# Stationary blocks of the expert stage stored column by column in interleaved rows

## The chip, the cores and the metric

The kernel runs on one core of one Trainium2 chip. The metric is the device time of one execution in microseconds, median of several runs; lower is better. One core has five engines with queues of their own: TensorE (PE, its weight loads listed apart as PEld), VectorE (DVE), ScalarE (ACT), GpSimd (POOL) and SyncE (SP), which here issues the large DMAs.

## What is computed

Two layers of a streaming encoder on 320 tokens (256 of a prompt, 64 of running streams), model width 1024. Each layer is a mixer (gated linear attention, a short convolution and differential attention, all fed by one projection) followed by a feed-forward part; the first layer's is dense, the second's is a mixture of eight experts, two for each token:

```python
D_MODEL, D_FF, N_EXPERTS, TOP_K, D_FF_E = 1024, 2816, 8, 2, 3584

def hybrid_layer(x, ...):
    xn = rmsnorm(x, g_mix)
    qa, ka, va, ga, ra, bb, cb, hb, qc, kc, vc = split_cols(xn @ w_in)
    ...
    x = x + jnp.concatenate([y_a, y_b, y_c], axis=-1) @ w_out
    x = x + ffn(rmsnorm(x, g_ffn))

def moe_ffn(x, w_r, wg, wu, wd):
    ...
    for e in range(N_EXPERTS):
        h = jax.nn.silu(xt @ wg[e]) * (xt @ wu[e])
        y = y + gates[:, e:e + 1] * jnp.dot(h, wd[e], preferred_element_type=F32)
```

All inputs and weights are float32.

## The kernel before, in words

**Precision.** A float32 product is made from three fast products (type `fp32r`, called FR in the code): each operand is split into a high part, which is the value rounded to that type, and a low part, which is the rest, and high x high, low x high and high x low are added in PSUM.

**The two halves of the program.** The first 570 us are the two mixers and the dense feed-forward part. There the weights are the stationary operand (128x128 blocks of `cut_hi` and `cut_lo`) and the 320 tokens stream past them. From about 577 us on, the experts run: there up to 128 tokens of one expert are stationary and the weights stream past them, 512 columns in one matmul.

**The expert stage.** One expert's weights come in 42 pieces (`NP`) of 128 x 2048 words: 28 of gate and up, then 14 of down. The program goes through experts in pairs, eight experts in all, 336 pieces. The SP queue fetches a piece (1 MB) into one of seven slots of `raw`; ACT writes the high part of it to one of three slots of `split_hi`; DVE writes the low part to `split_lo` and so frees the slot of `raw`; TensorE does 12 matmuls of 512 columns with it and then frees the slot of `split_hi` and `split_lo` for the piece three further on. Each of the 12 matmuls is preceded by the load of its 128x128 stationary block.

**The stationary blocks.** These are four tiles:

- `xgT_hi`, `xgT_lo`: the expert's tokens, transposed, in 8 blocks (`KB`) of 128 features. TensorE transposes the gathered rows `xg`, ACT writes each block of the high part with the gain (L1255), DVE the low part (L1823), 128 columns an instruction.
- `hmT_hi`, `hmT_lo`: the expert's activations, transposed, in 28 blocks (`FEB`). TensorE transposes four blocks at a time out of `hm` (L2528), ACT copies the 512 columns (L1303), DVE writes the low part (L1952).

```python
        hmT_hi = sb("hmT_hi", [P, FEB, P], FR)
        xgT_hi = sb("xgT_hi", [P, KB, P], FR)
        TE.matmul(o, xgT_hi[:, kk, :], hi[:, ...], start=kk == 0, stop=False)                          # L2475
        last = TE.transpose(tb[n % 2][:, 128 * k:128 * k + 128], hm[:, m % 2, k:512:4], ident)         # L2528
```

So the 128 columns of one stationary block stand side by side, 128 words in a row, in all four tiles. The transposes of `hm` are different: each takes every fourth column of `hm` as its stationary operand, while the transposes of `xg` (L1984) take 128 columns side by side.

**Lines.** Gate and up: L2475 is high block x high weights, L2479 low block x high weights, L2484 high block x low weights (and L2489 in the first piece). Down: L2510, L2513 and L2519 in the same sense, and L2495, L2496 and L2502 for an expert's last piece. Four instructions of the first part of the program are named further down: `warm`, 20 bfloat16 matmuls of 512 columns at the start; `xR,wr`, the router's product, whose stationary block has 8 columns; `Gown,x`, the first gather, float32 with 128 columns; and L1981, the weights of the first half.

**Order.** Each engine's order is written out by hand; a piece's steps wait on counters (`hi_ready`, `lo_ready`, `piece_used`, `t_full`, `th_ready`, `t_free`). TensorE is asked for a block of `hmT` four pieces before it needs it.

Of the kernel before, what the change touches and what calls it, by code (L numbers as in the profile page):

```python
# [25 lines left out]
P = 128  # L26
# [222 lines left out]
def build(nc, A, O):  # L249
# [5 lines left out]
    with ExitStack() as ctx:  # L255
# [162 lines left out]
        token_rows.close()  # L418
        hmT_hi = sb("hmT_hi", [P, FEB, P], FR)
        ye = sb("ye", [P, D])  # L420
# [36 lines left out]
        xg = sb("xg", [P, D])  # L457
        xgT_hi = sb("xgT_hi", [P, KB, P], FR)
        xgT_lo = sb("xgT_lo", [P, KB, P], FR)
        hs = sb("hs", [P, 2, 512])  # L460
# [3 lines left out]
        last_hot = sb("last_hot", [P, NT * P], FR)  # L464
        sb("below_hmT_lo", [P, 384])
        loop_only = ExitStack()
        hmT_lo = sb("hmT_lo", [P, FEB, P], FR, loop_only)
        loop_only.close()
# [96 lines left out]
        HALVES = [slice(0, 512), slice(512, 1024)]  # L565
        last_y_hi = xgT_hi[:].rearrange("p k n -> p (k n)")
        last_y_lo = xgT_lo[:].rearrange("p k n -> p (k n)")

# [315 lines left out]
        def _(act):  # L884
# [364 lines left out]
            def xg_hi(base, first, ks=range(KB)):  # L1249

                for k in ks:
                    if k % 4 == 0:
                        act.wait_ge(t_full, base + k // 4 + 1)
                    b = tb[(first + k // 4) % 2]
                    last = nc.scalar.activation(xgT_hi[:, k, :], b[:, 128 * (k % 4):128 * (k % 4) + 128], ACT.Copy, scale=gcol(3)[:, k:k + 1])  # L1255
                    if k % 4 == 3:
                        last.then_inc(th_ready, 1)
# [16 lines left out]
            def experts(count, ip, done):  # L1274

                for i in range(done, count * NP):
# [51 lines left out]
        def _(dve):  # L1328
# [488 lines left out]
            def xg_lo(first, base, ks=range(KB)):  # L1817

                for k in ks:
                    if k % 4 == 0:  # L1820
                        dve.wait_ge(th_ready, base + (first + k // 4 + 1))
                    b = tb[(first + k // 4) % 2]
                    last = V.scalar_tensor_tensor(out=xgT_lo[:, k, :], in0=b[:, 128 * (k % 4):128 * (k % 4) + 128], scalar=gcol(3)[:, k:k + 1],  # L1823
                                                  in1=xgT_hi[:, k, :].bitcast(F32), op0=ALU.mult, op1=ALU.subtract)
                    if k % 4 == 3:
                        last.then_inc(t_free, 1)
# [101 lines left out]
            def experts(count, ip, done):  # L1928

                for i in range(done, count * NP):  # L1930
# [45 lines left out]
        def _(pe):  # L1976
# [462 lines left out]
            def experts(count, ip, first=False):  # L2439

                for i in range(count * NP):
# [27 lines left out]
                    if j < 2 * FC:  # L2469
                        n, w = 4 // len(ms), 512 * len(ms)  # L2470
                        outs = [banks[2 * up + (FC * h + m) % 2][:] for m in ms]
                        for k in range(n):
                            kk = n * s + k
                            for c, o in enumerate(outs):
                                TE.matmul(o, xgT_hi[:, kk, :], hi[:, w * k + 512 * c:w * k + 512 * c + 512], start=kk == 0, stop=False)  # L2475
                            if first and i == 0:
                                continue
                            for c, o in enumerate(outs):
                                TE.matmul(o, xgT_lo[:, kk, :], hi[:, w * k + 512 * c:w * k + 512 * c + 512], start=False, stop=False)  # L2479
                        pe.wait_ge(lo_ready, ip * (2 * NP) + (i + 1 + PR))  # L2480
                        for k in range(n):
                            kk = n * s + k
                            for c, o in enumerate(outs):
                                last = TE.matmul(o, xgT_hi[:, kk, :], lo[:, w * k + 512 * c:w * k + 512 * c + 512], start=False, stop=kk == KB - 1)  # L2484
                        if first and i == 0:
                            pe.wait_ge(t_free, 1)
                            for k in range(n):
                                for c, o in enumerate(outs):
                                    last = TE.matmul(o, xgT_lo[:, k, :], hi[:, w * k + 512 * c:w * k + 512 * c + 512], start=False, stop=False)  # L2489
                    elif q == NP - 1:  # L2490
                        for n in range(2):
                            for k in range(2):
                                b = FEB - 2 + k
                                c = slice(1024 * k + 512 * n, 1024 * k + 512 * n + 512)
                                TE.matmul(banks[6 + n][:], hmT_hi[:, b, :], hi[:, c], start=False, stop=False)  # L2495
                                TE.matmul(banks[6 + n][:], hmT_lo[:, b, :], hi[:, c], start=False, stop=False)  # L2496
                            if n == 0:
                                pe.wait_ge(lo_ready, ip * (2 * NP) + (i + 1 + PR))
                            for k in range(2):
                                b = FEB - 2 + k  # L2500
                                c = slice(1024 * k + 512 * n, 1024 * k + 512 * n + 512)
                                last = TE.matmul(banks[6 + n][:], hmT_hi[:, b, :], lo[:, c], start=False, stop=k == 1)  # L2502
                            if n == 0:
                                last.then_inc(left_done, 1)
                    else:
                        for k in range(2):
                            b = 4 * (j - 2 * FC) + 2 * half + k
                            for n in range(2):
                                c = slice(1024 * k + 512 * n, 1024 * k + 512 * n + 512)
                                TE.matmul(banks[6 + n][:], hmT_hi[:, b, :], hi[:, c], start=b == 0, stop=False)  # L2510
                            for n in range(2):
                                c = slice(1024 * k + 512 * n, 1024 * k + 512 * n + 512)
                                TE.matmul(banks[6 + n][:], hmT_lo[:, b, :], hi[:, c], start=False, stop=False)  # L2513
# [93 lines left out]
```

## Time and profile before

| | |
|---|---|
| median of 3 runs | 1537.97 us (1537.42 to 1539.92) |
| the profiled execution, first to last instruction | 1535.8 us |
| PE busy | 1527.8 us, 99% of the span |
| DVE busy | 1234.4 us, 80% |
| ACT busy | 998.9 us, 65% |
| granted TensorE clock, mean | 0.997 |
| pieces of expert weights | 336 |
| matmuls recorded | 8428 |

The profile is of one execution. Its span runs from the first to the last instruction; it is 2.2 us shorter than the median of the runs, which also hold the start and the end of the program. PE's busy time counts overlapping matmuls once. The start of one matmul and the start of the next are what tells the pace; a single matmul is listed with about 390 ns because it is pipelined.

### The profile page before, as it was taken

To read this page: it belongs to the slowest core of one execution; us is meant where nothing else is said; L and a number is where in the kernel's file an instruction comes from. 1 tells how busy PE (TensorE), PEld (TensorE's weight loads), DVE (VectorE), ACT (ScalarE), POOL (GpSimd) and SP (SyncE) were. 2 spreads that over 40 slices of the span, in tenths; PEclk is the share of its full clock that TensorE was granted. 3 is DMA by queue.
4 is the path that set the end of the run, shared out by engine and by line. 5 is a ranking of instruction groups with operands and counts; after the bars stand their busy time and mean duration, and the time that the engine had idled before them with its cause. 6 is when DMAs were issued, how large, how long until landed. Compare 5 with 4: busy or idle time off the path is not lost.

```text
span 1535.8 us, 21611 instructions
## 1 busy us (share of the span) xinstructions
PE 1527.8 (99%) x8428; PEld 1333.0 (87%) x8428; DVE 1234.4 (80%) x1253; ACT 998.9 (65%) x1079; POOL 217.5 (14%) x249
## 2 busy tenths in 40 slices
PE   9999999999999999999999999999999999999998
PEld 7989999999998988888888888888888888888887
DVE  5877666654477758988988888998998988898897
ACT  5655433333466547777777778777777777777775
POOL 5514400001150403101001001002002002002000
PEclk9999999999999999999999999999999999999999
DMA  8333455444443459999999999999999999999994
GB/s 226 96 110 116 149 164 164 133 157 151 125 122 110 141 209 367 383 366 388 372 381 376 374 374 376 391 359 386 384 363 382 381 362 379 400 361 363 394 373 183
DMA packets 159701, 437.43 MB, mean 285 GB/s; under 512 B 12068, under 2 KB 66176, under 8 KB 145264
## 3 DMA queue, kind: packets, MB, share of 16 engines
q1 hardware_dynamic: 151796, 423.02, 75.0%
q0 software_dynamic: 5552, 9.62, 2.3%
q10 hardware_dynamic: 2252, 3.41, 0.7%
q8 instruction: 68, 1.11, 0.3%
q14 instruction: 33, 0.27, 0.1%
HBM read 429.40 MB, written 13.60 MB: 288 GB/s over the span
## 4 chain that ended last, share of the span: by engine, by line
PE 98%; DMA 0%; ACT 0%; DVE 0%; issue 0%; SPq 0%; DVEq 0%; ACTq 0%
PE bank L1981 34%; PE bank L2475 13%; PE bank L2484 13%; PE bank L2479 13%; PE bank L2510 6%; PE bank L2513 6%; PE bank L2519 6%; PE bank L1984 3%; PE bank L2528 2%; PE bank L2496 0%; PE bank L2502 0%; PE bank L2495 0%; DMA gla<-b_g 0%; DVE x L1972 0%; ACT L1076 0%
## 5 line engine op out<-in xcount | busy, mean ns | idle before, releaser
L1808 DVE TENSOR_TENSOR split_lo<-raw,split_hi 128x2048 fp32r<-128x2048 f32 x336 | 763.1, 2289 | 101.8 <-ACT split_hi L1207 100.8
L1207 ACT CAST split_hi<-raw 128x2048 fp32r<-128x2048 f32 x336 | 640.5, 1911 | 224.5 <-PE bank L2484 145.7
L2475 PE MATMUL bank<-split_hi,xgT_hi 128*128 128x512 f32 x896 | 291.7, 395 | 0.0
L2479 PE MATMUL bank<-split_hi,xgT_lo 128*128 128x512 f32 x892 | 285.8, 390 | 0.0
L2484 PE MATMUL bank<-split_lo,xgT_hi 128*128 128x512 f32 x896 | 239.9, 390 | 0.0
L913 ACT CAST cut_hi<-ring 128x1024 fp32r<-128x1024 f32 x124 | 129.9, 1048 | 166.6 <-PE bank L1981 166.6
L1981 PE MATMUL bank<-xT_hi,cut_hi 128*128 128x320 f32 x752 | 236.7, 315 | 0.0
L1981 PE MATMUL bank<-xT_hi,cut_lo 128*128 128x320 f32 x752 | 233.5, 310 | 0.0
L1981 PE MATMUL bank<-xT_lo,cut_hi 128*128 128x320 f32 x752 | 231.9, 308 | 0.0
L1346 DVE TENSOR_TENSOR cut_lo<-ring,cut_hi 128x1024 fp32r<-128x1024 f32 x124 | 153.0, 1235 | 80.7 <-ACT cut_hi L913 79.9
L2484 PEld LDWEIGHTS bank<-split_lo,xgT_hi 128*128 128x128 f32 x896 | 168.3, 188 | 34.9
L2479 PEld LDWEIGHTS bank<-split_hi,xgT_lo 128*128 128x128 f32 x892 | 167.7, 188 | 34.7
L2475 PEld LDWEIGHTS bank<-split_hi,xgT_hi 128*128 128x128 f32 x896 | 166.2, 189 | 32.3
L1981 PEld LDWEIGHTS bank<-xT_hi,cut_hi 128*128 128x128 f32 x752 | 142.1, 189 | 1.6
L1981 PEld LDWEIGHTS bank<-xT_lo,cut_hi 128*128 128x128 f32 x752 | 142.2, 189 | 0.0
L1981 PEld LDWEIGHTS bank<-xT_hi,cut_lo 128*128 128x128 f32 x752 | 142.0, 189 | 0.0
L2510 PE MATMUL bank<-split_hi,hmT_hi 128*128 128x512 f32 x416 | 129.8, 393 | 0.0
L2513 PE MATMUL bank<-split_hi,hmT_lo 128*128 128x512 f32 x416 | 128.3, 390 | 0.0
L2519 PE MATMUL bank<-split_lo,hmT_hi 128*128 128x512 f32 x416 | 111.3, 390 | 0.0
L853 POOL COPY idc<-idx 128x1 uint32 (+1 forms) x8 | 5.7, 707 | 635.9 <-PE bank L1984 616.0
L2513 PEld LDWEIGHTS bank<-split_hi,hmT_lo 128*128 128x128 f32 x416 | 78.2, 188 | 16.3
L2519 PEld LDWEIGHTS bank<-split_lo,hmT_hi 128*128 128x128 f32 x416 | 78.1, 188 | 16.2
(316 smaller groups left out, 1723.2 us busy)
## 6 DMA issues: line engine op xcount, KB each, us to landing
raw<-moe_w_gate SPq DMA_DIRECT2D x112, 1024.0 KB, 7.8
raw<-moe_w_up SPq DMA_DIRECT2D x112, 1024.0 KB, 7.6
raw<-moe_w_down SPq DMA_DIRECT2D x112, 1024.0 KB, 7.3
ring<-w_in SPq DMA_DIRECT2D x15, 1024.0 KB, 5.5
ring<-ffn_w_gate SPq DMA_DIRECT2D x11, 1024.0 KB, 5.5
ring<-ffn_w_up SPq DMA_DIRECT2D x11, 1024.0 KB, 5.4
ring<-ffn_w_down SPq DMA_DIRECT2D x10, 1024.0 KB, 5.1
ring<-w_out SPq DMA_DIRECT2D x8, 1024.0 KB, 5.0
```

The source lines that it names most:

```text
L913: nc.scalar.copy(split_cut(cut_hi, q), raw_cut(q)).then_inc(cut_hi_ready, 1)
L1207: return nc.scalar.copy(split_hi[:, i % SR, :], raw_piece(i)).then_inc(hi_ready, 1)
L1346: V.tensor_tensor(split_cut(cut_lo, q), raw_cut(q), split_cut(cut_hi, q).bitcast(F32), ALU.subtract).then_inc(cut_lo_ready, 1)
L1808: V.tensor_tensor(split_lo[:, i % SR, :], raw_piece(i), split_hi[:, i % SR, :].bitcast(F32), ALU.subtract).then_inc(lo_ready, 1)
L1981: return TE.matmul(out, lhsT, rhs, start=start, stop=stop)
L1984: return TE.transpose(out, in_, ident[0:rows, 0:rows])
L2475: TE.matmul(o, xgT_hi[:, kk, :], hi[:, w * k + 512 * c:w * k + 512 * c + 512], start=kk == 0, stop=False)
L2479: TE.matmul(o, xgT_lo[:, kk, :], hi[:, w * k + 512 * c:w * k + 512 * c + 512], start=False, stop=False)
L2484: last = TE.matmul(o, xgT_hi[:, kk, :], lo[:, w * k + 512 * c:w * k + 512 * c + 512], start=False, stop=kk == KB - 1)
L2510: TE.matmul(banks[6 + n][:], hmT_hi[:, b, :], hi[:, c], start=b == 0, stop=False)
L2513: TE.matmul(banks[6 + n][:], hmT_lo[:, b, :], hi[:, c], start=False, stop=False)
L2519: last = TE.matmul(banks[6 + n][:], hmT_hi[:, b, :], lo[:, c], start=False, stop=b == FEB - 1)
```

## The change

The four tiles of stationary blocks become two, and the two axes of each are exchanged: the index of the block is now the inner one. `spread` has 128 rows of 62 words; words 0 to 7 of a row are column n of the eight blocks of `xgT_hi`, words 8 to 15 those of `xgT_lo`, words 16 to 43 those of the 28 blocks of `hmT_lo`, and 18 words of each row are not used. `spread_hi` has 128 rows of 30 words, 28 of which are column n of the blocks of `hmT_hi`. A load of a stationary block so takes 128 words that stand 62 or 30 words (248 or 120 bytes) apart. ACT and DVE write the blocks, and DVE reads the high ones back, with the same distances. The numbers of instructions, their order on every engine, their semaphores and the operands' sizes stay the same; only names and addresses differ. `last_y`, which lay over `xgT_hi` and `xgT_lo`, gets a tile of its own.

```diff
-        hmT_hi = sb("hmT_hi", [P, FEB, P], FR)
+        spread_hi = sb("spread_hi", [P, P, 30], FR)
...
-        xgT_hi = sb("xgT_hi", [P, KB, P], FR)
-        xgT_lo = sb("xgT_lo", [P, KB, P], FR)
+        last_y = sb("last_y", [P, 2, D], FR)
...
-        hmT_lo = sb("hmT_lo", [P, FEB, P], FR, loop_only)
+        spread = sb("spread", [P, P, 62], FR, loop_only)
...
+        def xgT_hi(k):
+            return spread[:, :, 0 + k]
+
+        def xgT_lo(k):
+            return spread[:, :, 8 + k]
+
+        def hmT_hi(b):
+            return spread_hi[:, :, 0 + b]
+
+        def hmT_lo(b):
+            return spread[:, :, 16 + b]
+
+        HMT_HI, HMT_LO = (spread_hi, 0), (spread, 16)
+
+        def four(part, j):
+            tile, first = part
+            return tile[:, :, first + 4 * j:first + 4 * j + 4].rearrange("p n s -> p s n")
+
+        def four_in(bank):
+            return bank[:].rearrange("p (s n) -> p s n", s=4)
...
-                    last = nc.scalar.activation(xgT_hi[:, k, :], b[:, 128 * (k % 4):128 * (k % 4) + 128], ACT.Copy, scale=gcol(3)[:, k:k + 1])
+                    last = nc.scalar.activation(xgT_hi(k), b[:, 128 * (k % 4):128 * (k % 4) + 128], ACT.Copy, scale=gcol(3)[:, k:k + 1])
...
-                        nc.scalar.copy(hmT_hi[:, 4 * j:4 * j + 4, :].rearrange("p b n -> p (b n)"), tb[n % 2][:]).then_inc(th_ready, 1)
+                        nc.scalar.copy(four(HMT_HI, j), four_in(tb[n % 2])).then_inc(th_ready, 1)
...
-                        V.tensor_tensor(hmT_lo[:, 4 * j:4 * j + 4, :].rearrange("p b n -> p (b n)"), tb[n % 2][:],
-                                        hmT_hi[:, 4 * j:4 * j + 4, :].rearrange("p b n -> p (b n)").bitcast(F32), ALU.subtract).then_inc(t_free, 1)
+                        V.tensor_tensor(four(HMT_LO, j), four_in(tb[n % 2]), four(HMT_HI, j).bitcast(F32), ALU.subtract).then_inc(t_free, 1)
...
-                                TE.matmul(o, xgT_hi[:, kk, :], hi[:, w * k + 512 * c:w * k + 512 * c + 512], start=kk == 0, stop=False)
+                                TE.matmul(o, xgT_hi(kk), hi[:, w * k + 512 * c:w * k + 512 * c + 512], start=kk == 0, stop=False)
...
-                                last = TE.matmul(banks[6 + n][:], hmT_hi[:, b, :], lo[:, c], start=False, stop=b == FEB - 1)
+                                last = TE.matmul(banks[6 + n][:], hmT_hi(b), lo[:, c], start=False, stop=b == FEB - 1)
```

The other matmuls of the stage change in the same way.

## Rows read from the trace of the kernel before

**Rows 1.** The page: engines' busy us (share of the span) xinstructions
```profile
PE 1527.8 (99%) x8428; PEld 1333.0 (87%) x8428; DVE 1234.4 (80%) x1253; ACT 998.9 (65%) x1079; POOL 217.5 (14%) x249
```

**Rows 2.** The page: chain of work that ended last, shares by line
```profile
PE bank L1981 34%; PE bank L2475 13%; PE bank L2484 13%; PE bank L2479 13%; PE bank L2510 6%; PE bank L2513 6%; PE bank L2519 6%; PE bank L1984 3%; PE bank L2528 2%; PE bank L2496 0%; PE bank L2502 0%; PE bank L2495 0%; DMA gla<-b_g 0%; DVE x L1972 0%; ACT L1076 0%
```

**Rows 3.** The page's groups: operation, count, busy us, mean ns, idle before and releaser
```profile
L1808 DVE TENSOR_TENSOR split_lo<-raw,split_hi 128x2048 fp32r<-128x2048 f32 x336 | 763.1, 2289 | 101.8 <-ACT split_hi L1207 100.8
...
L2475 PE MATMUL bank<-split_hi,xgT_hi 128*128 128x512 f32 x896 | 291.7, 395 | 0.0
...
L2484 PEld LDWEIGHTS bank<-split_lo,xgT_hi 128*128 128x128 f32 x896 | 168.3, 188 | 34.9
```

**Rows 4.** Timeline of PE, 899.9 to 906.2 us: start us, length us, operation
```profile
899.95 0.62 PE L2510 MATMUL bank<-split_hi,hmT_hi 128*128 128x512 f32 x2
...
902.67 0.62 PE L2510 MATMUL bank<-split_hi,hmT_hi 128*128 128x512 f32 x2
```

**Rows 5.** Timeline of PE, 5.95 to 6.0 and 7.60 to 7.62 us
```profile
5.67 0.59 PE L1981 MATMUL bank<-warm 128*128 128x512 bf16 x2
...
7.39 0.38 PE L1981 MATMUL bank<-warm 128*128 128x512 bf16 x1
```

**Rows 6.** Timelines: loads at 561.3 and at 571 us, matmuls at 300 us
```profile
561.32 0.09 PEld L1981 LDWEIGHTS bank<-xR,wr 128*8 128x8 f32 x1 [0.18 <-issue]
...
563.20 0.09 PEld L1981 LDWEIGHTS bank<-xR,wr 128*8 128x8 f32 x1 [0.18 <-issue]
...
570.88 1.20 PEld L1981 LDWEIGHTS bank<-Gown,x 128*128 128x128 f32 x10
...
299.81 0.31 PE L1981 MATMUL bank<-xT_hi,cut_lo 128*128 128x320 f32 x1
...
300.97 0.31 PE L1981 MATMUL bank<-xT_lo,cut_hi 128*128 128x320 f32 x1
```

**Rows 7.** Line L1981: loads by operands, ns min/median/max, first and last start
```profile
L1981 PEld LDWEIGHTS bank<-xT_hi,cut_hi x752: 186/188/331, 14.9 to 527.9; 128*128 128x128 f32 x188
...
L1981 PEld LDWEIGHTS bank<-Gown,x x48: 183/192/193, 570.3 to 576.1; 128*128 128x128 f32 x32, 64*128 64x128 f32 x16
...
L1981 PEld LDWEIGHTS bank<-warm x20: 97/114/152, 1.2 to 7.2; 128*128 128x128 bf16 x20
...
L1981 PEld LDWEIGHTS bank<-xR,wr x18: 85/90/91, 560.8 to 569.6; 128*8 128x8 f32 x18
```

**Rows 8.** Transposes of xg and of hm: timeline around 679 and 905 us
```profile
679.09 1.03 PEld L1984 LDWEIGHTS bank<-const_sb,xg 128*128 128x128 f32 x8
679.32 1.03 PE L1984 MATMUL bank<-const_sb,xg 128*128 128x128 f32 x8
...
905.17 0.67 PEld L2528 LDWEIGHTS bank<-const_sb,hm 128*128 128x128 f32 x4
905.40 0.63 PE L2528 MATMUL bank<-const_sb,hm 128*128 128x128 f32 x4
```

**Rows 9.** Lines L1984 and L2528: those loads and transposes, ns min/median/max
```profile
L1984 PEld LDWEIGHTS bank<-const_sb,xg x64: 138/140/143, 679.1 to 1511.1; 128*128 128x128 f32 x64
L1984 PE MATMUL bank<-const_sb,xg x64: 270/273/273, 679.3 to 1511.2; 128*128 128x128 f32 x64
...
L2528 PEld LDWEIGHTS bank<-const_sb,hm x224: 195/208/220, 604.5 to 1499.3; 128*128 128x128 f32 x112
L2528 PE MATMUL bank<-const_sb,hm x224: 270/283/386, 604.7 to 1499.4; 128*128 128x128 f32 x112
```

**Rows 10.** Groups of 600 to 1500 us: the writers of the blocks
```profile
L1952 DVE TENSOR_TENSOR hmT_lo<-bank,hmT_hi 128x512 fp32r<-128x512 f32 x55 | 37.6, 684 | 0.0
...
L1823 DVE SCALAR_TENSOR_TENSOR xgT_lo<-bank,pcol,xgT_hi 128x128 fp32r<-128x128 f32 x56 | 15.1, 343 | 0.0
```

**Rows 11.** 600 to 1500 us: busy PE, PEld, DVE, ACT, POOL; clock, DMA share, GB/s
```profile
600.00:1500.00 900.00, 899.97 (x4097) 749.72 (x4096) 804.74 (x493) 683.17 (x505) 67.59 (x60) 1.00 1.00 377
```

**Rows 12.** The SP queue's waits, 600 to 1535 us: in total, times, longest us
```profile
SPq L648 <- DVE split_lo L1808: 785.1, 320, 3.9
```

More of the change, by code:

```diff
@@ L464, in build @@
         last_hot = sb("last_hot", [P, NT * P], FR)
-        sb("below_hmT_lo", [P, 384])
+        sb("below_spread", [P, 320])
         loop_only = ExitStack()
-        hmT_lo = sb("hmT_lo", [P, FEB, P], FR, loop_only)
+        spread = sb("spread", [P, P, 62], FR, loop_only)
         loop_only.close()
@@ L565, in build @@
         HALVES = [slice(0, 512), slice(512, 1024)]
-        last_y_hi = xgT_hi[:].rearrange("p k n -> p (k n)")
-        last_y_lo = xgT_lo[:].rearrange("p k n -> p (k n)")
+        last_y_hi, last_y_lo = last_y[:, 0], last_y[:, 1]
+        def xgT_hi(k):
[12 more added lines that the diff above has]
+            return bank[:].rearrange("p (s n) -> p s n", s=4)
         def y_rows_of(t, c):
@@ L1822, in xg_lo @@
                     b = tb[(first + k // 4) % 2]
-                    last = V.scalar_tensor_tensor(out=xgT_lo[:, k, :], in0=b[:, 128 * (k % 4):128 * (k % 4) + 128], scalar=gcol(3)[:, k:k + 1],
-                                                  in1=xgT_hi[:, k, :].bitcast(F32), op0=ALU.mult, op1=ALU.subtract)
+                    last = V.scalar_tensor_tensor(out=xgT_lo(k), in0=b[:, 128 * (k % 4):128 * (k % 4) + 128], scalar=gcol(3)[:, k:k + 1],
+                                                  in1=xgT_hi(k).bitcast(F32), op0=ALU.mult, op1=ALU.subtract)
                     if k % 4 == 3:
@@ L2478, in experts @@
                             for c, o in enumerate(outs):
-                                TE.matmul(o, xgT_lo[:, kk, :], hi[:, w * k + 512 * c:w * k + 512 * c + 512], start=False, stop=False)
+                                TE.matmul(o, xgT_lo(kk), hi[:, w * k + 512 * c:w * k + 512 * c + 512], start=False, stop=False)
                         pe.wait_ge(lo_ready, ip * (2 * NP) + (i + 1 + PR))
@@ L2483, in experts @@
                             for c, o in enumerate(outs):
-                                last = TE.matmul(o, xgT_hi[:, kk, :], lo[:, w * k + 512 * c:w * k + 512 * c + 512], start=False, stop=kk == KB - 1)
+                                last = TE.matmul(o, xgT_hi(kk), lo[:, w * k + 512 * c:w * k + 512 * c + 512], start=False, stop=kk == KB - 1)
                         if first and i == 0:
@@ L2488, in experts @@
                                 for c, o in enumerate(outs):
-                                    last = TE.matmul(o, xgT_lo[:, k, :], hi[:, w * k + 512 * c:w * k + 512 * c + 512], start=False, stop=False)
+                                    last = TE.matmul(o, xgT_lo(k), hi[:, w * k + 512 * c:w * k + 512 * c + 512], start=False, stop=False)
                     elif q == NP - 1:
@@ L2494, in experts @@
                                 c = slice(1024 * k + 512 * n, 1024 * k + 512 * n + 512)
-                                TE.matmul(banks[6 + n][:], hmT_hi[:, b, :], hi[:, c], start=False, stop=False)
-                                TE.matmul(banks[6 + n][:], hmT_lo[:, b, :], hi[:, c], start=False, stop=False)
+                                TE.matmul(banks[6 + n][:], hmT_hi(b), hi[:, c], start=False, stop=False)
+                                TE.matmul(banks[6 + n][:], hmT_lo(b), hi[:, c], start=False, stop=False)
                             if n == 0:
@@ L2501, in experts @@
                                 c = slice(1024 * k + 512 * n, 1024 * k + 512 * n + 512)
-                                last = TE.matmul(banks[6 + n][:], hmT_hi[:, b, :], lo[:, c], start=False, stop=k == 1)
+                                last = TE.matmul(banks[6 + n][:], hmT_hi(b), lo[:, c], start=False, stop=k == 1)
                             if n == 0:
@@ L2509, in experts @@
                                 c = slice(1024 * k + 512 * n, 1024 * k + 512 * n + 512)
-                                TE.matmul(banks[6 + n][:], hmT_hi[:, b, :], hi[:, c], start=b == 0, stop=False)
+                                TE.matmul(banks[6 + n][:], hmT_hi(b), hi[:, c], start=b == 0, stop=False)
                             for n in range(2):
                                 c = slice(1024 * k + 512 * n, 1024 * k + 512 * n + 512)
-                                TE.matmul(banks[6 + n][:], hmT_lo[:, b, :], hi[:, c], start=False, stop=False)
+                                TE.matmul(banks[6 + n][:], hmT_lo(b), hi[:, c], start=False, stop=False)
                         pe.wait_ge(lo_ready, ip * (2 * NP) + (i + 1 + PR))
```

## The prediction

> **What bounds the kernel now.** I read the engines' busy time first [rows 1], then the chain of work that ended last [rows 2], then the groups [rows 3]. PE is busy for 99% of the span, nearly the whole chain is PE's lines, and its expert lines L2475, L2479, L2484, L2510, L2513, L2519 make up 57% of it. No matmul group shows idle time before it. In the expert stage, 600 to 1500 us, PE is busy for 899.97 of 900 us at a granted clock of 1.00, which is 2.4 GHz; DVE is busy for 804.74 us and ACT for 683.17 us [rows 11]. The DMAs wait for DVE to free slots, not the other way round: SP's queue waited 785.1 us for split_lo [rows 12]. So the time of this stage is the number of matmuls times their pace, and only a change of that pace, or something that becomes slower than it, moves the end.
>
> **The pace.** The timeline shows a piece's first matmul at 899.95 us and the next piece's first at 902.67 us, 12 matmuls later [rows 4]: 2.72 / 12 = 226.7 ns each. There are 336 pieces (the count of L1808 [rows 3]), so 336 x 12 = 4032 such matmuls, 914 us of the 1535.8 us of the profiled execution. That execution is 2.2 us under the median of 1537.97 us; I take differences from its rows and put them to the median.
>
> **What the pace consists of.** Streaming 512 columns at one column in a cycle of 2.4 GHz is 213.3 ns, so 13.4 ns of each pitch are something else. Three rows say what kind of thing. (a) The bfloat16 matmuls at the start, 512 columns too, come every (7.39 - 5.67) / 8 = 215 ns [rows 5]; their 128-column loads last 114 ns, where a load of the experts lasts 188 ns [rows 3, 7]. (b) `xR,wr` is a plain float32 matmul of 320 columns with an 8-column load (90 ns [rows 7]) and comes every (563.20 - 561.32) / 7 = 268.6 ns [rows 6], which is two cycles a column, 266.7 ns, plus 2. (c) `Gown,x` is a plain float32 one of 128 columns with a 128-column load of 192 ns [rows 7]: (1.20 - 0.19) / 9 = 112.2 ns [rows 6], two cycles a column, 106.7 ns, plus 5.5. The first half's matmuls, which stream as fast as the experts' and load 128 columns in 188 ns, come every (300.97 - 299.81) / 8 = 145 ns for 320 columns [rows 6, 7]: 133.3 plus 11.7, so the addition does not shrink or grow with the length of the stream. It cannot be a wait for the load, either: at 145 ns the next matmul begins before a load's recorded 188 ns are over, and at 226.7 ns there are 82 ns more. The addition is thus 2 ns with a short or a quick load, 5.5 ns with a full one beside a stream that reads at half pace, and 12 to 13 with a full one beside a stream that reads a word in every cycle. I read this as the load and the stream getting in each other's way in SBUF, some 11 ns for each load; no row shows the collision itself.
>
> **The change, part by part.**
>
> The loads. 4032 loads read 128 words 62 or 30 words apart. What that does to a load that is covered by a stream of 512 columns is the whole question. The address walk is arithmetic. A load of 8 columns lasts 90 ns and one of 128 columns 188 [rows 7], 98 / 120 = 0.82 ns a column, in which time the stream moves by two words. Side by side, the columns move by one word, so the two reads drift against each other and meet again and again. In the first case the distance between the two reads stands still, and at most one collision is left. Neither the banks nor the order of columns is in any row, so I bound the gain: at best the pace becomes that of (a), 215.0 ns, which is 11.7 ns less and 4032 x 11.7 = 47.2 us; at worst it is nothing. I take 217.5 ns, the 215.0 of the quick load plus 2.5 ns, between (a) and (c), since some loads will begin in a bad phase: 9.2 ns x 4032 = 37.1 us.
>
> Against a load being slow in itself: the transposes of `hm` load every fourth column, 4 words apart, those of `xg` side by side, otherwise they are alike. The first last 208 ns at the median and the second 140 [rows 9], and a transpose comes every (630 - 283) / 3 = 116 ns instead of (1030 - 273) / 7 = 108 [rows 8]; the 283 and 273 ns are the lengths of one [rows 9]. So distance makes a load about 68 ns longer. But where such a load lies under a matmul of 512 columns it costs nothing: in both places the last big matmul has the first load beside it, which starts at 905.17 or 679.09, and the first transpose starts 0.23 us later, at 905.40 or 679.32. A load of 188 + 68 = 256 ns whose first 90 ns or so are latency (the 8-column load's 90 [rows 7]) holds its port for about 170 ns, under 217.5. So I cost the length of the loads at nothing; what hides it is the stream, with 48 ns to spare. The Trainium skill, page "SBUF — State Buffer", section "SBUF: two separate sides", holds that lines are 16 bytes and that an access which goes to a new line each time pays a penalty, for float32 from a distance of 4 words on. The longer loads of `hm` agree with it; that the cover takes it up is what those two starts show. Its sections on ports also say that the load and the stream have a read port each and take nothing from each other; by that the 11 ns would not be a collision and the change would give nothing, which is the second rival.
>
> The writers. DVE writes `hmT_lo` 56 times at 684 ns, with its second input spread as well, and `xgT_lo` 64 times at 343 ns [rows 10], where 55 and 56 of them lie in the window. ACT writes the high blocks as often, and has 217 of 900 us free [rows 11]. No row shows DVE or ACT with words so far apart. Bounds: nothing, or each word twice as long, which is 512 x 1.04 = 533 ns more for a `hmT_lo` and 133 for a `xgT_lo` (1.04 ns from L1808: 2289 ns for 2048 words with its fixed part, at most 1.12). That is 56 x 0.53 + 64 x 0.13 = 38 us of DVE in the stage. At today's pace DVE has 900 - 805 = 95 us free there, so it hides; at the new one 58 us are free, and it still does on average. I take nothing. PE asks for a block four pieces (10.9 us) before it uses it, which covers another 0.5 us twice. The added tile `last_y` moves nothing.
>
> What else could be late next. At 217.5 ns a piece takes 2.61 us, and DVE needs 2.29 us of that for the piece alone. The transposes lengthen the round for both. DMA would have to move 377 x 900 / 863 = 393 GB/s instead of 377 [rows 11]. The share of 1.00 there is no limit by itself, since the queue waits for slots; but 4% more is not shown to be free.
>
> Sum: 1537.97 - 37.1 = 1500.9 us.
>
> **The rivals.**
>
> 1. Gain, but held back. DVE's or DMA's share above becomes real: the writers at twice the time, or DMA stuck near 385 GB/s, give 900 x 377 / 385 = 881 us for the window instead of 863, or only one of the two tiles gets into step. Roughly half of the gain, 1519 us. For it: DVE at 805 of 900 us. Against it: 100.8 of the 101.8 us that it idles before a split are waits for ACT [rows 3], none for a DMA.
>
> 2. No change. The 11 ns belong to the handing over of the blocks and not to the addresses, as the page's ports say; the loads stay hidden as those of `hm` do. 1538 us. For it: the equal 0.23 us in rows 8, in which a spread load costs the stream no more and no less than one side by side. That row speaks against my forecast too; but 4 words are not the same walk as -2, and 10 ns cannot be read from two starts in steps of 10.
>
> 3. Slower. Each column now lies in a 16-byte line of its own, 128 lines instead of 32, and the load takes from the stream what those lines cost. The place is every one of the 4032 matmuls. Price: the 8 ns by which the transposes of `hm` are slower than those of `xg` [rows 8] give 4032 x 8 = 32 us, 1570 us; if the 11 ns were paid per line, 44 instead of 11, it would be 133 us, 1671 us. It decides as soon as the pace rises above 227.5 ns. The Trainium skill's line rule, taken as binding for a covered load, gives this case.
>
> **How the numbers follow.** The forecast, 1490 to 1512 us, has a chance of 0.50; the first rival, 1512 to 1534, of 0.17; no change 0.15; slower 0.18. The range that holds 8 in 10 goes from the best bound, 1537.97 - 47.2 = 1490.8, to just above no change, 1541; the forecast's own is 1490 to 1512. A measurement of this kernel tells about 0.2% (3 us, 0.76 ns a matmul) from no change. So faster 0.67, same 0.15, slower 0.18.
>
> **What would show it.** In the timeline of the changed kernel, twelve matmuls from one piece's first to the next one's: 2.61 us for the forecast, 2.72 for no change, 2.73 and more for slower. The first half, up to 570 us, stays as it is to a few tenths of a microsecond; if it moves, the comparison is off. The loads' length says whether distance is felt (188 before, 250 or so by rows 9). `hmT_lo` at 684 ns or at 1.2 us settles the writers. If PE shows idle time before its expert lines, released by DVE or by a DMA, the first rival holds. A pace between 222 and 227 would mean that the walk of addresses matters, but not as I think; a pace of 227 with loads of 250 ns would mean that there was no collision to remove.

## The result: 81 us slower

The changed kernel takes 1619.14 us, median of 4 runs (1617.98 to 1621.49); the kernel before, on the same chip, 1537.93 us (1537.42 to 1539.92). The ratio is 1.0533, 95% interval 1.0518 to 1.0548. That is 81.2 us more, where I had said 37 us less. The profiled execution spans 1616.5 us.

The page of the changed kernel first, its engines' busy time and then the groups (operation, count, busy us, mean ns, idle before), which answer to [rows 1, 3]:

```profile
PE 1608.4 (100%) x8428; PEld 1570.6 (97%) x8428; DVE 1273.7 (79%) x1253; ACT 1033.1 (64%) x1079; POOL 218.0 (13%) x249
...
L2493 PE MATMUL bank<-split_hi,spread 128*128 128x512 f32 x896 | 312.6, 418 | 0.0
...
L2493 PEld LDWEIGHTS bank<-split_hi,spread 128*128 128x128 f32 x896 | 264.2, 332 | 0.1
...
L2502 PEld LDWEIGHTS bank<-split_lo,spread 128*128 128x128 f32 x896 | 239.6, 333 | 0.0
```

The matmuls' lines are still never idle, so nothing outside TensorE holds them up. What changed is the loads: 333 ns instead of 188, and the 34.9 us in which PEld stood idle before L2484 are gone. The busy windows (busy us of PE, PEld, DVE, ACT, POOL; clock, DMA share, GB/s) say the same of the whole stage:

```profile
600.00:1500.00 900.00, 900.00 (x3767) 898.63 (x3767) 772.89 (x455) 658.97 (x468) 67.13 (x59) 1.00 0.95 347
0.00:570.00 570.00, 566.20 (x4053) 532.45 (x4054) 380.22 (x692) 273.95 (x530) 133.77 (x173) 1.00 0.46 145
```

PEld is now busy for 898.6 of 900 us, before for 749.7 [rows 11]. DVE, ACT and the DMAs all have more room than before, and the clock is the same, 1.00. The second window is the first half, which the change doesn't touch; its PE is busy as long as that of the kernel before:

```profile
0.00:570.00 570.00, 566.32 (x4040) 533.01 (x4040) 378.86 (x689) 271.98 (x527) 133.28 (x172) 0.99 0.45 143
```

So the 81 us lie in the stage of the experts. Its pace is in the timeline of PE (start us, length us), from one piece's first matmul to the next one's:

```profile
901.06 0.66 PE L2493 MATMUL bank<-split_hi,spread 128*128 128x512 f32 x2
...
904.02 0.65 PE L2493 MATMUL bank<-split_hi,spread 128*128 128x512 f32 x2
```

Twelve in 2.96 us are 246.7 ns each; over all neighbouring matmuls of the stage, without those that stand beside a transpose, the mean is 246.0 ns, against 227.1 in the kernel before. 4032 x 18.9 = 76 us. The rest is at the transposes, in the step from the first big matmul behind them to the second. The timeline of the changed kernel and then that of the kernel before:

```profile
912.86 0.63 PE L2546 MATMUL bank<-const_sb,hm 128*128 128x128 f32 x4
...
913.25 0.60 PE L2493 MATMUL bank<-split_hi,spread 128*128 128x512 f32 x1
...
913.69 0.41 PE L2497 MATMUL bank<-split_hi,spread 128*128 128x512 f32 x1
```

```profile
905.79 0.71 PE L2510 MATMUL bank<-split_hi,hmT_hi 128*128 128x512 f32 x2
906.33 0.63 PE L2513 MATMUL bank<-split_hi,hmT_lo 128*128 128x512 f32 x2
```

From the first to the second big matmul it is 0.44 us now, and was 0.54 - 0.23 = 0.31 us. That is 0.13 us, of which 0.02 are in the pace already, at 56 places (224 transposes of `hm` in fours [rows 9]): 6 us. Together 82 us, for 81.2 measured. Where the time went is thus accounted for; the experiments ask why the pace is 246.

### The profile page after: what moved, and what is told of

Read it like the earlier page. It is cut to its first block, busy times and chain, and to the rows that moved or that the text cites. A ratio compares the mean times of both kernels' runs of the same rounds, so it can differ in the third digit from the quotient of the medians.

```text
span 1616.5 us, 21611 instructions
## 1 busy us (share of the span) xinstructions
PE 1608.4 (100%) x8428; PEld 1570.6 (97%) x8428; DVE 1273.7 (79%) x1253; ACT 1033.1 (64%) x1079; POOL 218.0 (13%) x249
## 4 chain that ended last, share of the span: by engine, by line
PE 98%; ACT 0%; DVE 0%; DMA 0%; issue 0%; SPq 0%; DVEq 0%; ACTq 0%
PE bank L1999 32%; PE bank L2493 14%; PE bank L2502 14%; PE bank L2497 14%; PE bank L2528 6%; PE bank L2537 6%; PE bank L2531 6%; PE bank L2002 2%; PE bank L2546 2%; PE bank L2514 0%; PE bank L2513 0%; PE bank L2520 0%; DMA gla<-b_g 0%; DVE x L1990 0%; ACT cut_hi L932 0%
## 5 line engine op out<-in xcount | busy, mean ns | idle before, releaser
L2493 PE MATMUL bank<-split_hi,spread 128*128 128x512 f32 x896 | 312.6, 418 | 0.0
L2497 PE MATMUL bank<-split_hi,spread 128*128 128x512 f32 x892 | 301.6, 408 | 0.0
L2493 PEld LDWEIGHTS bank<-split_hi,spread 128*128 128x128 f32 x896 | 264.2, 332 | 0.1
L2497 PEld LDWEIGHTS bank<-split_hi,spread 128*128 128x128 f32 x892 | 263.5, 332 | 0.0
L2502 PE MATMUL bank<-split_lo,spread 128*128 128x512 f32 x896 | 257.1, 409 | 0.0
L2502 PEld LDWEIGHTS bank<-split_lo,spread 128*128 128x128 f32 x896 | 239.6, 333 | 0.0
L2528 PE MATMUL bank<-split_hi,spread_hi 128*128 128x512 f32 x416 | 139.0, 416 | 0.0
L2531 PE MATMUL bank<-split_hi,spread 128*128 128x512 f32 x416 | 136.7, 410 | 0.0
L2528 PEld LDWEIGHTS bank<-split_hi,spread_hi 128*128 128x128 f32 x416 | 120.9, 334 | 0.0
L2531 PEld LDWEIGHTS bank<-split_hi,spread 128*128 128x128 f32 x416 | 120.2, 333 | 0.0
L2537 PE MATMUL bank<-split_lo,spread_hi 128*128 128x512 f32 x416 | 120.0, 411 | 0.0
L2537 PEld LDWEIGHTS bank<-split_lo,spread_hi 128*128 128x128 f32 x416 | 112.1, 334 | 0.0
```

Of the source, the lines that this page charges most:

```text
L2493: TE.matmul(o, xgT_hi(kk), hi[:, w * k + 512 * c:w * k + 512 * c + 512], start=kk == 0, stop=False)
L2497: TE.matmul(o, xgT_lo(kk), hi[:, w * k + 512 * c:w * k + 512 * c + 512], start=False, stop=False)
L2502: last = TE.matmul(o, xgT_hi(kk), lo[:, w * k + 512 * c:w * k + 512 * c + 512], start=False, stop=kk == KB - 1)
L2528: TE.matmul(banks[6 + n][:], hmT_hi(b), hi[:, c], start=b == 0, stop=False)
L2531: TE.matmul(banks[6 + n][:], hmT_lo(b), hi[:, c], start=False, stop=False)
L2537: last = TE.matmul(banks[6 + n][:], hmT_hi(b), lo[:, c], start=False, stop=b == FEB - 1)
```

## The experiments

The first theory (A in the expectations) is that a load whose columns lie in different lines takes longer than a matmul of 512 columns, so that the loads set the pace. Its rivals are that load and stream disturb each other in SBUF, each being short enough by itself (B), and that the slower writers take the time (C). The kernels that stream or load only part of their columns (half_side, half_spread, quarter_side, half_two, the surveys, narrow) were run once each; the other times are medians of 4 runs, that of writers of 10. The kernel before took 1537.3 to 1537.4 us beside them. Where kernels name `xh_tile`, `xl_tile`, `hh_tile` and `hl_tile`, these stand for `xgT_hi`, `xgT_lo`, `hmT_hi` and `hmT_lo`, held in rows of so many words each; a row of one word is the layout of the kernel before.

### Half the stream, with both layouts

Each matmul of the experts streams 256 of its 512 columns, once with the blocks side by side (half_side), once with the changed kernel's blocks (half_spread):

```diff
-TE.matmul(o, xgT_hi(kk), hi[:, w * k + 512 * c:w * k + 512 * c + 512], start=kk == 0, stop=False)
+TE.matmul(o[:, 256 * (kk % 2):256 * (kk % 2) + 256], xgT_hi(kk), hi[:, w * k + 512 * c:w * k + 512 * c + 256], start=kk == 0, stop=False)
```

> The blocks stand side by side as before, but each of the 4032 expert matmuls streams 256 of its 512 columns (even blocks into the left half of the bank, odd blocks into the right), so half of the product is left out; the loads are all there. Both theories expect the same: 106.7 ns of stream plus the 13.4 ns of before, so a matmul every 120 ns within a piece, loads of 188 ns. The time is then set by DVE (2.29 us a piece): some 1460 to 1500 us.

> The changed kernel with the same halved streams: half of the product is left out, the loads are all there and spread over rows of 62 and 30 words. Theory A, the load is the bound (a spread load holds its path for about 246 ns, more than the stream needs): the pace does not care for the stream, a matmul every 246 ns, time about 1615 us. Theory B, each load takes its toll from the stream (13.4 ns side by side, 33 ns spread): a matmul every 106.7 + 33 = 140 ns, and DVE sets the time, 1460 to 1500 us. Theory C, the slow writers: 120 ns within a piece.

The first took 1469.09 us, the second 1605.52 us. The timelines of PE, half_side and then half_spread:

```profile
906.22 0.40 PE L2499 MATMUL bank<-split_hi,xh_tile 128*128 128x256 f32 x2
...
907.65 0.40 PE L2499 MATMUL bank<-split_hi,xh_tile 128*128 128x256 f32 x2
```

```profile
899.79 0.65 PE L2493 MATMUL bank<-split_hi,spread 128*128 128x256 f32 x2
...
902.73 0.41 PE L2493 MATMUL bank<-split_hi,spread 128*128 128x256 f32 x1
```

With the blocks side by side, twelve matmuls take 1.43 us, 119 ns each, half of the columns and nearly half of the time. (That kernel's total is not 4032 x 107 ns lower, because PE then waits for pieces, and because its clock was lower in part of the stage; see the last section.) With spread blocks they take 2.94 us, 245 ns each, although only half as much streams. A matmul of 256 columns has nothing that lasts 245 ns but its load. So the load sets the pace; a disturbance between the two would have shrunk with the stream. What the stream still adds in the changed kernel is 246.0 - 244.5 = 1.5 ns by the means. Only behind the transposes of `hm` does the length of the stream show: the step from the first big matmul to the second is 0.32 us in half_spread and 0.44 in the changed kernel (medians of 56 places), 0.12 us more for 107 ns more of stream. There load and stream stand one behind the other, so nearly all of the longer load is paid.

### A quarter of the stream: the own pace of a load side by side

The layout of the kernel before, 128 of 512 columns streamed:

```diff
+TE.matmul(o[:, 128 * (kk % 4):128 * (kk % 4) + 128], xgT_hi(kk), hi[:, w * k + 512 * c:w * k + 512 * c + 128], start=kk == 0, stop=False)
```

> Blocks side by side, each matmul streams only 128 of its 512 columns (three quarters of the product are left out), so that the load is longer than the stream. It gives a load's own pace: 128 columns at 0.82 ns are 105 ns, so a matmul comes every 105 to 120 ns. If it comes every 67 ns (53.3 + 13.4), the load is no bound even here.

It took 1505.02 us. Two stretches of its timeline, and its windows:

```profile
640.43 1.05 PE L2508 MATMUL bank<-split_lo,xh_tile 128*128 128x128 f32 x4
641.29 0.41 PE L2499 MATMUL bank<-split_hi,xh_tile 128*128 128x128 f32 x1
...
908.00 0.38 PE L2534 MATMUL bank<-split_hi,hh_tile 128*128 128x128 f32 x2
...
909.34 0.38 PE L2534 MATMUL bank<-split_hi,hh_tile 128*128 128x128 f32 x2
```

```profile
600.00:700.00 100.00, 98.37 (x462) 97.90 (x463) 91.70 (x66) 75.89 (x59) 15.18 (x11) 0.50 1.00 386
...
908.00:911.00 3.00, 3.00 (x29) 3.00 (x29) 1.97 (x2) 2.75 (x5) 2.84 (x3) 1.00 1.02 410
```

Most of the stage ran at a granted clock of 0.50, 1.2 GHz, which I had not expected (see the last section). In the stretch at 908 us the clock is 1.00, and twelve matmuls take 1.34 us, 111.7 ns each, of which the stream needs 53. So 111.7 ns is the own pace of a load of 128 columns side by side: two cycles a column and 5 ns. At 1.2 GHz it is 0.86 / 4 = 215 ns, two cycles a column again. That of `Gown,x`, 112.2 ns, was the same number [rows 6]; in the prediction I put it down to a slow stream. That row alone can't tell the two apart, since 128 columns of stream at two cycles each give the same. Another row of the kernel before can: `own,Gown` loads 128 columns and streams only 2, and its second and third matmuls start 0.11 us apart. The timelines of PE at 584.95 to 585.0 and at 585.06 to 585.1 us:

```profile
584.80 0.36 PE L1981 MATMUL bank<-own,Gown 128*128 128x2 f32 x2
...
584.91 0.36 PE L1981 MATMUL bank<-own,Gown 128*128 128x2 f32 x2
```

So it is the load. A spread load's own pace is 245 ns by half_spread, 1.04 ns more for each column.

### How far apart: rows of 2 and 4 words

All four tiles in rows of 4 words (four_words) or of 2 (two_words), with full streams. `k // 4` and `k % 4` become `k // 2` and `k % 2` in the second:

```diff
-        spread_hi = sb("spread_hi", [P, P, 30], FR)
+        hh_tile = sb("hh_tile", [P, 7, P, 4], FR)
...
-            return spread[:, :, 0 + k]
+            return xh_tile[:, k // 4, :, k % 4]
```

> Blocks interleaved in fours: rows of 4 words, all four tiles, so each load reads words 16 bytes apart, as the transposes of hm do; each column in a 16-byte line of its own, as in the changed kernel. If lines are what costs (A with the price by the line): loads of 333 ns, a matmul every 246 ns, 1619 us. If the exact distance (62 and 30 words) costs, and 4 words cost only the 68 ns that the transposes of hm show: loads of 256 ns, the pace stays at 227 ns, 1538 us. Theory C: 1619 us if the writers take 1.2 us here too.

> All four tiles interleaved in pairs: rows of 2 words, so a load finds two of its columns in each 16-byte line, the two others belong to the neighbouring block. If the cost is by lines (side by side 32 lines; 4 words apart 128 lines, 310 ns): 64 lines, the load stays within 190 to 230 ns, which the stream covers; a matmul every 227 ns, 1538 us. If any distance from one word on costs the full price: loads of 310 ns, a matmul every 235 ns, 1575 us as with four words.

Rows of 4: 1575.51 us, ratio 1.0250 (1.0233 to 1.0267). Rows of 2: 1561.94 us, ratio 1.0164 (1.0147 to 1.0181). Neither came as expected. Rows of 4 lie between the two times given: the loads are long, but at 311 ns not as long as in the changed kernel, and the mean pace is 235.2 ns. Rows of 2 have loads as short as the first case wanted and are slower all the same. One tile's loads in each (ns min/median/max), four_words and then two_words, and a piece of the timeline of two_words:

```profile
L2503 PEld LDWEIGHTS bank<-split_hi,xl_tile x892: 308/311/332, 578.2 to 1522.4; 128*128 128x128 f32 x179
```

```profile
L2503 PEld LDWEIGHTS bank<-split_hi,xl_tile x892: 192/193/200, 577.9 to 1508.9; 128*128 128x128 f32 x179
```

```profile
1002.66 0.63 PE L2499 MATMUL bank<-split_hi,xh_tile 128*128 128x512 f32 x2
...
1005.46 0.40 PE L2499 MATMUL bank<-split_hi,xh_tile 128*128 128x512 f32 x1
```

The load's length jumps between 2 and 4 words, from 193 to 311 ns. At 2 words two columns share 16 bytes, at 4 each has its own. The Trainium skill, page "SBUF — State Buffer", section "SBUF: two separate sides", says of its 16-byte lines that "each access that crosses to a new line pays a penalty", and that two accesses in a line avoid it. The loads' lengths agree. But the pace at 2 words is not that of the kernel before: twelve take 2.80 us, 233.3 ns each, 6.7 ns more. This the length of the load does not explain.

### Rows of 2 words with half the stream

> Rows of 2 words in all four tiles with halved streams (half of the product is left out). With full streams the loads lasted 193 ns and a matmul came every 233.5 ns, 6.7 more than side by side. If the load were the bound there too, the pace stays at 233 ns. If the doubled lines of the load cost the stream 6.7 ns, or the change of block does, it is 120 + 6.7 = 127 ns.

The edits of two_words and half_side together (half_two) took 1466.20 us, as little as half_side. Two pairs of one of its pieces:

```profile
1000.88 0.40 PE L2534 MATMUL bank<-split_hi,hh_tile 128*128 128x256 f32 x2
...
1001.36 0.40 PE L2534 MATMUL bank<-split_hi,hh_tile 128*128 128x256 f32 x2
```

Four in 0.48 us, 120 ns each, neither of the two paces expected. With half the stream the 6.7 ns are gone, or at most 1 is left (median 120 ns within the pieces, as in half_side). They need a full stream of 512 columns beside the load, while the load is far from setting the pace. A disturbance between load and stream is thus real, but small, and at 2 words it is there where side by side it is not. What it is stays open.

### Does the distance itself matter? Two surveys at half stream

With half the stream the load's own pace is bare, so one kernel can read four distances, one for each tile. survey_a: 8, 9, 28 and 5 words for `xh`, `xl`, `hh` and `hl`; survey_b: 16, 17, 32 and 4. Two of the lines of survey_b, against half_side:

```diff
-        xh_tile = sb("xh_tile", [P, 8, P, 1], FR, loop_only)
+        xh_tile = sb("xh_tile", [P, 1, P, 16], FR, loop_only)
...
-        hh_tile = sb("hh_tile", [P, 28, P, 1], FR)
+        hh_tile = sb("hh_tile", [P, 1, P, 32], FR)
```

> Halved streams again (half of the product is left out), with four distances at once: high features 8 words, low features 9, high activations 28, low activations 5. Price by lines alone: every one is a line of its own for each column, so all loads last 310 to 345 ns and a matmul comes every 232 to 246 ns. If the distance matters beyond that, through banks, the odd ones (5, 9) and the even ones (8, 28) differ by more than 10 ns.

> Halved streams (half of the product is left out): high features 16 words, low features 17, high activations 32, low activations 4. By lines alone: 310 to 345 ns for all, 4 words the same 310 as before. If banks matter, 32 words (each column at the same place in 128 bytes) are the slowest by far, 400 ns or more.

They took 1578.94 and 1530.77 us. The loads, survey_a and then survey_b:

```profile
L2503 PEld LDWEIGHTS bank<-split_hi,xl_tile x892: 334/339/345, 579.9 to 1527.8; 128*128 128x128 f32 x179
...
L2534 PEld LDWEIGHTS bank<-split_hi,hh_tile x416: 301/322/333, 661.4 to 1564.4; 128*128 128x128 f32 x139
```

```profile
L2499 PEld LDWEIGHTS bank<-split_hi,xh_tile x896: 291/316/322, 576.4 to 1479.6; 128*128 128x128 f32 x180
...
L2534 PEld LDWEIGHTS bank<-split_hi,hh_tile x416: 294/318/327, 656.5 to 1516.4; 128*128 128x128 f32 x139
```

The median step from one matmul to the next of the same tile is 242, 243, 228 and 228 ns in survey_a, 222, 222, 226 and 233 in survey_b. All distances from 4 words up are in one band, twice the 111.7 ns of side by side; the distances move the pace inside it by some 20 ns. Odd and even distances don't part as the expectation of survey_a asked. 32 words, where banks that repeat would be hit again and again, is among the quickest, and not at 400 ns. So the first term is the line of its own, and my arithmetic on multiples of 32 has no support here. Why 8 and 9 words are slower than 16 and 17 I can't say, nor why the 30 words of the changed kernel's high blocks (245 ns in half_spread) are slower than 28 and 32.

### Rows of 16 and 32 words with the full stream

The quickest distances, features in rows of 16 and activations in rows of 32 words, with full streams (sixteen). If the pace were the larger of load and stream, it would be 227 to 230 ns.

> Full streams with the distances whose loads were the quickest in the surveys: features in rows of 16 words, activations in rows of 32 (222 to 226 ns from load to load). If only the load's own pace counts, it stays under the 227 ns of the stream and handing over: 1538 us, as before. If a spread load also takes something from the stream (6.7 ns at 2 words), 233 ns a matmul, 1564 us; if what it takes adds to what it holds, 1575 to 1600 us.

It took 1586.19 us, ratio 1.0323 (1.0303 to 1.0344), more than rows of 4 words and in the range of the third case. The mean pace is 238.0 ns, where loads at these distances ran at 222 to 226 ns beside half streams. So here a full stream adds something to a spread load that is about as long as itself. "The larger of the two" is not the whole rule: it is nearly right where the load is far longer (the changed kernel, 245 against 227: 246), and 11 ns short here. That the two are close does not explain it either: rows of 4 words are close too, 233 (survey_b) against 227, and four_words ran at 235.2, only 2 ns more.

### Only one of the four tiles spread

Only the high activation blocks in rows of 30 words (high_only), as the changed kernel has them; the other three side by side.

```diff
+        hh_tile = sb("hh_tile", [P, 1, P, 30], FR)
+        hl_tile = sb("hl_tile", [P, 28, P, 1], FR, loop_only)
```

> One part of the change alone: only the high activation blocks are spread, in rows of 30 words; the other three tiles stand side by side. These blocks are loaded 8 times in each of the 112 down pieces, 896 loads of 4032. Load-bound theory: each of these loads makes its matmul come after 246 ns instead of 227, the others stay; 896 x 19 = 17 us, 1555 us. The down matmuls that are followed by a load of a low block stay at 227 ns.

1561.03 us, ratio 1.0157 (1.0140 to 1.0174). Its loads by tile, `hh` and `hl`:

```profile
L2534 PEld LDWEIGHTS bank<-split_hi,hh_tile x416: 318/332/345, 657.7 to 1545.7; 128*128 128x128 f32 x139
```

```profile
L2537 PEld LDWEIGHTS bank<-split_hi,hl_tile x416: 187/190/206, 658.2 to 1546.2; 128*128 128x128 f32 x139
```

23.7 us for 896 spread loads are 26 ns each, more than the 19 ns of the pace: from a high block's matmul to a low one's, whose own load is short, it is 243 ns on average, and between two low ones 232, both above 227. The gate and up matmuls of the same kernel, whose loads are not spread, stay at 227 ns. The cost goes with the loads that are spread and sits where they are, and in part on the low blocks' matmuls beside them, which were expected to stay at 227.

### Only the writers

The loads read tiles side by side; from the second expert on, ACT and DVE write (and DVE reads back) the activation blocks in a tile `aside` with rows of 34 words, which TensorE does not read (writers).

```diff
-                        nc.scalar.copy(four(HMT_HI, j), four_in(tb[n % 2])).then_inc(th_ready, 1)
+                        once = done and h == 0
+                        nc.scalar.copy(four(HMT_HI, j) if once else beside(HMT_HI, j), four_in(tb[n % 2])).then_inc(th_ready, 1)
```

> All loads side by side as before. Only the writing is spread: after the first expert ACT and DVE write the activation blocks into a tile aside, in rows of 34 words, which TensorE does not read (it goes on with the first expert's blocks, so the later experts' down product is wrong). Theories A and B: the writers take 1.2 us instead of 0.58 and 0.68 and are hidden, 1538 us within 3. Theory C, the slow writers hold TensorE up: 1600 us or more.

1536.69 us, ratio 0.9999 (0.9989 to 1.0008). The groups of the changed kernel from 600 to 1600 us, then those of writers from 700 to 1450 us:

```profile
L1971 DVE TENSOR_TENSOR spread<-bank,spread_hi 128x512 fp32r<-128x512 f32 x56 | 67.1, 1198 | 0.0
...
L1322 ACT CAST spread_hi<-bank 128x512 fp32r<-128x512 f32 x56 | 66.2, 1183 | 0.0
```

```profile
L1330 ACT CAST aside<-bank 128x512 fp32r<-128x512 f32 x44 | 51.6, 1172 | 0.0
...
L1980 DVE TENSOR_TENSOR aside<-bank,aside 128x512 fp32r<-128x512 f32 x44 | 50.8, 1155 | 0.0
```

The writers are nearly as slow as in the changed kernel, 2.0 times the 579 ns and 1.7 times the 684 ns of before, and the time stays. The writers of the activation blocks are not the cause, and the prediction's "hidden" holds for them. The shorter ones of the feature blocks were not spread in this run.

### A shorter load side by side

Gate and up matmuls load, and so compute, only 64 of the 128 token columns; down matmuls are left alone (narrow). If load and stream met in SBUF, as I had read the 13.4 ns, half the columns should take half of it away.

```diff
+TE.matmul(o[0:64], xgT_hi(kk)[:, 0:64], hi[:, w * k + 512 * c:w * k + 512 * c + 512], start=kk == 0, stop=False)
```

> All blocks side by side, full streams. The gate and up matmuls load and compute only 64 of the 128 tokens' columns (the upper 64 tokens are left out); the down matmuls are untouched and serve as the measure. If the 13.4 ns that a matmul takes beyond its 213.3 ns of stream are taken by the load, column by column (the reading of the prediction), the gate and up matmuls come every 220 ns and the down ones every 227. If they are a fixed price of changing the block, both come every 227 ns. The time is 1538 us in the second case and about 1520 in the first.

1542.94 us. Its loads of the low blocks, and a piece's timeline:

```profile
L2503 PEld LDWEIGHTS bank<-split_hi,xl_tile x892: 133/134/137, 578.1 to 1492.1; 128*64 128x64 f32 x179
```

```profile
1000.19 0.63 PE L2499 MATMUL bank<-split_hi,xh_tile 128*64 128x512 f32 x2
...
1002.95 0.40 PE L2499 MATMUL bank<-split_hi,xh_tile 128*64 128x512 f32 x1
```

The load is 54 ns shorter, and the pace is 2.76 / 12 = 230 ns, not less than 227 (the down matmuls of the same kernel stay at 227; where the 3 ns come from is not known). The 13.4 ns are no price per column of the load. half_side says the same from the other side: with 256 columns streamed the pace is 106.7 + 13 ns. It acts as a fixed price of each matmul of this kind, and the collisions along the load, which the change was to remove, are not there. What the 13.4 ns are stays open.

## Why the prediction was wrong, point by point

**The bound** was read rightly: the stage is matmuls times pace, and 4032 times the change of pace gives 76 of the 81 us, the places at the transposes 6 more. DVE, ACT and DMA never became the bound.

**The step that failed: the length of the loads, costed at nothing with 48 ns to spare.** The transposes' loads are 68 ns longer when spread [rows 9]. I added these 68 ns to the 188 of an ordinary load and took 90 off for latency, so 170 ns. Measured: 333 ns long, an own pace of 245. Subtracting about 90 was good (333 ns long at a pace of 246 in the changed kernel, 342 at 245 in half_spread: 87 and 97); adding a difference was not. A transpose's load is a quicker one, 140 ns against 188, with (140 - 90) / 128 = 0.4 ns a column where the ordinary load has 98 / 120 = 0.82. Spread, it takes 118 / 50 = 2.4 times as long beyond its 90 ns. The same ratio on the ordinary load's 98 ns gives 231 ns, above the forecast pace of 217.5 and above today's 227: no spare at all. The rows to see it were there, since the prediction itself quotes both 140 and 188. The ratio is itself no law, as the transposes' pace rose only from 108 to 116 ns.

**The evidence for the cover** was the equal 0.23 us from load to first transpose [rows 8]. It was taken at the first transpose only, whose load has an own pace of 116 ns at most (a transpose comes every 116 ns) and a whole stream to hide under. It says nothing of a load whose own pace is 245 ns.

**The gain** (9.2 ns a matmul) rested on reading 11 of the 13.4 ns as collisions. narrow speaks against that reading, and the surveys leave the walk of addresses without support. I had written that no row shows the collision, and still gave it half of the chance.

**The rivals.** The third, slower by one line for each column, has the right sign and the right place, with 0.18. That its sizes, 8 and 33 ns, enclose the 19 measured, and 1570 and 1671 us the 1619, is luck: both prices were of something the load takes from the stream, whereas it is mostly the load's own length. The line rule of the Trainium skill that I cited against my forecast (page "SBUF — State Buffer", section "SBUF: two separate sides") is borne out: 2 words apart the loads last 193 ns, 4 words apart 311. The same page's section "Who interferes with whom" says that TensorE has two read ports, one for the stream and one for the loads, independent of each other. This gave the second rival, and narrow agrees with it; but two_words and sixteen show 7 and 11 ns that come with a full stream, and there the measurement decides. The page gives no price for either.

**What would show it.** Twelve matmuls in 2.73 us or more meant slower, and 2.96 came. `hmT_lo` at 1.2 us was the upper bound of the writers' cost (533 ns more), and 1198 against 684 came, 514 more. The loads, by my rows 250 ns, came at 333.

**Left open:** what the full stream adds to a load in rows of 2 words (6.7 ns) and of 16 or 32 (11 ns above the longer of the two) and hardly at 4; why distances from 4 words up differ by 20 ns; what the 13.4 ns are. A distance of 3 words, where some neighbours share a line, was not run. None of the layouts tried beats the kernel before, whose blocks stand side by side; it stays the best.

## What to carry to other kernels

Keep the columns of a stationary block side by side: at every distance from 4 words up that was run here (4 to 62), its load costs twice as much, and a matmul of 512 columns hides it no longer or only just. Whether a load is hidden is not read from its recorded length but from its own pace, and a kernel with halved streams shows that directly. When a price comes from a neighbouring operation, ask first whether that operation has the same base; if not, give both the difference and the ratio, and let the range hold both.

## What the runs showed of the chip that I had not expected

- **The clock fell while PE was busy.** In quarter_side the granted clock was 1.00 from 540 to 576 us with PE busy for 35.2 of 36 us, then 0.74 from 576 to 590 us with PE busy for 11.1 of 14, and 0.50 (1.2 GHz) from 590 us on for most of the stage, with PE busy for 97 to 98% of it in matmuls of 128 columns behind loads of 128. With 256 columns streamed (half_side) the mean clock was 0.944, with PE busy for 71 to 76% of each 100 us of the stage; with 512 it is 0.997. At the lower clock a matmul of quarter_side took 213 ns instead of 112, and the kernel took 1505.02 us against half_side's 1469.09, though it streams half as much.
- **Writers pay for lines, too.** 512 words written by ACT and by DVE took 579 and 684 ns side by side, 619 and 684 in rows of 2 words, 1095 and 1108 in rows of 4, 1183 and 1198 in the changed kernel.
- **A quick load can be hurt by its neighbour.** In high_only, matmuls with a low block, whose loads are side by side and 190 ns long, start 232 to 243 ns after the one before; where no tile is spread it is 227.
